# A diffusion step with product-key experts: three small groups of work change their place in a hand-written order

## The reference, cut to what matters

```python
def layer(x, cond, h0_f, h0_b, rows, p):
    ...
    y, h_f, h_b = token_mixer(h, h0_f, h0_b, rows, p)     # w_in, SSM | conv, rms norm per conv head, w_out
    x = x + g1 * y
    h = rmsnorm(x, p["norm2_g"]) * (1 + sc2) + sh2
    x = x + g2 * peer(h, p["w_query"], p["sub_keys"], p["expert_u"], p["expert_v"])

def block(xb):                                            # 128 tokens, 8 heads, 16 experts of each
    q = (xb @ w_query).astype(jnp.float32).reshape(TOKEN_BLOCK, PEER_HEADS, 2, PEER_DQ // 2)
    s = jnp.einsum("thse,sne->thsn", q, sk)
    ...                                                   # two top-16 of 128 keys, then top 16 of 256 sums
    hid = jnp.einsum("thkd,td->thk", expert_u[idx], xb).astype(jnp.float32)
    act = (jax.nn.gelu(hid) * gate).astype(xb.dtype)
    return jnp.einsum("thk,thkd->td", act, expert_v[idx])
```

## Time and profile before

| | |
|---|---|
| median of 3 runs | 1960.12 us |
| the three runs | 1955.56, 1960.12, 1962.29 us |
| span of the profiled execution, first to last instruction | 1954.5 us |
| own time of the profiled execution | not given apart from its span; the lowest run lies 1.1 us above the span, the median 5.6 us |
| busy: PE, DVE, ACT, POOL | 1197.1, 1423.2, 373.2, 717.9 us |
| moved by DMA | 745.91 MB, of them 671.13 MB by the gathers' queue |

### The profile page before, as it was taken

How to read it: one execution, slowest core, us unless ns; L and a number is a source line. 1 busy time by engine, 2 the same in 40 slices (tenths; PEclk the granted TensorE clock), 3 DMA queues, 4 the chain that set the end, 5 groups by cost and what they waited for, 6 DMA issues and landing times.

```text
span 1954.5 us, 22601 instructions
## 1 busy us (share of the span) xinstructions
PE 1197.1 (61%) x7716; PEld 476.1 (24%) x7716; DVE 1423.2 (73%) x3894; ACT 373.2 (19%) x845; POOL 717.9 (37%) x666
## 2 busy tenths in 40 slices
PE   6999888999767767774553434453444454444434
PEld 3569544444322322220110000111000011111001
DVE  8978557777766776667777777777777678877775
ACT  5242431221122111111211011121111111211010
POOL 0000233333333333334444444444444444344442
PEclk9999999999878777775755555565555565555555
DMA  8556799999999999999999999999999999999996
GB/s 347 179 196 220 275 358 401 373 396 415 401 368 374 404 414 401 397 401 393 421 421 422 419 410 416 412 412 412 416 413 415 417 412 415 415 410 419 412 409 254
DMA packets 126243, 745.91 MB, mean 382 GB/s; under 512 B 12128, under 2 KB 34912, under 8 KB 40624
## 3 DMA queue, kind: packets, MB, share of 16 engines
q0 software_dynamic: 92160, 671.13, 83.8%
q1 hardware_dynamic: 33968, 73.35, 10.5%
HBM read 741.78 MB, written 2.65 MB: 381 GB/s over the span
## 4 chain that ended last, share of the span: by engine, by line
DMA 33%; PE 30%; DVE 24%; issue 10%; ACT 1%; SPq 0%; DVEq 0%; POOL 0%; POOLq 0%; ACTq 0%
DMA r<-table,gidx 29%; DVE r L1707 8%; PE bank L846 7%; PE bank L814 6%; PE bank L951 3%; DMA r<-w_query 3%; PE bank L964 2%; PE bank L543 2%; DMA r<-w_u 2%; PE bank L781 1%; DVE wgt L1719 1%; DVE i L1649 1%; DVE r L1675 1%; DVE i L1655 1%; DVE r L1650 1%
## 5 line engine op out<-in xcount | busy, mean ns | idle before, releaser
L1890 POOL DMA_INDIRECT r<-table,gidx x640 | 709.7, 1109 | 1053.1 <-PE bank L846 891.0
L1707 DVE CUSTOM_DVE_ANT_0 r<-r 128x1024 f32<-128x1024 f32 x640 | 780.3, 1225 | 310.4 <-DMA r<-table,gidx 292.8
L846 PE MATMUL bank<-r,wgt 128*32 128x512 f32 x2560 | 532.2, 916 | 711.3 <-DVE wgt L1719 692.2
L846 PEld LDWEIGHTS bank<-r,wgt 128*32 128x32 f32 x2560 | 61.3, 130 | 1078.5 <-DVE wgt L1719 1011.3
L1258 ACT ACTIVATE r<-r 128x2 f32<-128x2 f32 x320 | 65.1, 204 | 1033.3 <-DVE r L1707 1016.4
L814 PE MATMUL bank<-hT_r,r 128*128 128x512 f32 x256 | 120.1, 624 | 0.9 <-ACT hT_r L1112 0.9
L1716 DVE TENSOR_TENSOR r<-r 128x2 f32<-128x2 f32 x320 | 50.1, 157 | 68.5 <-ACT r L1258 68.5
L1719 DVE TENSOR_TENSOR wgt<-fold,r 128x64 f32<-128x64 f32 x320 | 72.0, 225 | 11.1
L814 PEld LDWEIGHTS bank<-hT_r,r 128*128 128x128 f32 x256 | 50.0, 200 | 75.1 <-issue 75.1
L1258 ACT ACT_TABLE_LOAD x51 | 65.4, 1283 | 0.9
L964 PE MATMUL bank<-mix_r,r 128*128 128x512 f32 x128 | 61.0, 619 | 0.0
(11 more groups left out here) (356 smaller groups left out, 1438.5 us busy)
## 6 DMA issues: line engine op xcount, KB each, us to landing
r<-w_mod SPq DMA_DIRECT2D x24, 1024.0 KB, 8.2
r<-w_query SPq DMA_DIRECT2D x15, 1024.0 KB
r<-table,gidx POOLq DMA_INDIRECT x640, 11.7
r<-w_tiles SPq DMA_DIRECT2D x12, 512.0 KB, 8.2
x_r<-w_tiles SPq DMA_DIRECT2D x10, 512.0 KB, 5.9
hT_r<-xT SPq DMA_DIRECT2D x4, 640.0 KB, 5.9
r<-w_u SPq DMA_DIRECT2D x1, 2048.0 KB, 29.9
r<-w_o SPq DMA_DIRECT2D x1, 2048.0 KB, 10.9
```

The costliest lines, as they stand in the source:

```text
L846: last = mm(bank[ACC[b % 2][h]][to:to + TG, :], wgt[:, g % 2, e, :], rows[:, k % SLOTS, D + h * 512:D + (h + 1) * 512], start=(G % HEADS = ...
L1707: V.tensor_tensor_reduce(rows[:, s, 0:D], rows[:, s, 0:D], h2r[tg], 1.0, 0.0, ALU.mult, ALU.add, hid[:, par, k:k + 1]).then_inc(dot_done, 1)
L1890: G_.indirect_dma_start(rows[:, k % SLOTS, :], None, table, bass.IndirectOffsetOnAxis(gidx[:, e, k:k + 1], 0)).then_inc(row_in[k % SLOTS], 16)
```

## The change

There are three edits, all within the first block's heads.

1. On PE the conv heads' sums of squares (positions 12, 18, 24, 30) come ahead of the position's products of the projection instead of behind them.
2. On PE, for G of 1 to 5, the two halves of a query stand at g = 2 and 3 instead of 3 and 4, and the scores at g = 5 instead of 6. For G = 0 they stay.
3. On ACT the copy of the queries (g = 5) comes behind the position's gelu instead of ahead of it. The copy of the scores moves from ahead of the gelu of g = 6 to behind the gelu of g = 7.

```diff
@@ PE, latent_front(n)
+                if n in (12, 18, 24, 30):
+                    i = (n - 12) // 6
+                    pe.wait_ge(sql_ready, 5 + i)
+                    pe.wait_ge(mixl_ready, i + 1)
+                    for j in range(4):
+                        last = mm(bank[6][:, 2 * j:2 * j + 2], sql[i % 2][:, j * P:(j + 1) * P], headones[:, 0:P:64], start=True, stop=True)
+                    last.then_inc(sql_used, 1)
                 if n == 9:
                     spread_columns(0)
                 if n in (13, 19, 25, 31):
...
                     if half:
                         last.then_inc(zl_mm, 1)
-                if n in (12, 18, 24, 30):
-                    i = (n - 12) // 6
-                    pe.wait_ge(sql_ready, 5 + i)
-                    pe.wait_ge(mixl_ready, i + 1)
-                    for j in range(4):
-                        last = mm(bank[6][:, 2 * j:2 * j + 2], sql[i % 2][:, j * P:(j + 1) * P], headones[:, 0:P:64], start=True, stop=True)
-                    last.then_inc(sql_used, 1)
@@ PE, the loop over heads and positions
                     if u < HEADS:
-                        if g in (3, 4):
-                            query(u, (g - 3,))
-                        if g == 6:
+                        early = 1 if G else 0
+                        if g + early in (3, 4):
+                            query(u, (g + early - 3,))
+                        if g + early == 6:
                             scores(u)
@@ ACT, the loop over heads and positions
+                    gelu(G, e, g)
                     if u < HEADS:
                         if g == 5:
                             take_q(u)
-                        if g == 6:
+                        if g == 7:
                             take_scores(u)
-                    gelu(G, e, g)
```

## The result

The changed kernel takes 1970.81 us, the median of 9 runs (1962.04 to 1975.60). The kernel before takes 1959.51 us beside it, also 9 runs (1950.79 to 1962.44). The ratio is 1.0056, with a 95% interval of 1.0039 to 1.0072: 11 us slower, 7.6 to 14. The forecast of 1960 us was wrong, and 1970.8 lies above its range. It also lies above the 1967 us of the rival that ends slower.

A forecast was written before the change was run, and what follows sets the result against it. The gathers' DMA at 416 GB/s was taken as the bound, PE almost a second. Terms -3.5 - 1.0 + 4.7 + 0 = +0.2 us on a span of 1954.5 gave 1954.7; plus 5.6 to the median, about 1960 us, range 1952.5 to 1968.

The forecast's parts named there:

- Position 10: Query for G = 1: PE waits 3 to 5 us for its load, costing about 0, at worst 2 us.
- Position 26: Query for G = 3: PE waits 6.0 us for its load, then slow matmuls; net 4.7 us lost, bounds 0 and 8.
- position 3: Case in before's trace: PE waited 4.98 us for a query's load, matmuls took 3.78 us, DMA lost 6.6 us.
- Slow matmuls behind a wait: At position 26 the query's matmuls after the wait run on the slow clock, adding 1.8 us on PE.
- Edits 1 and 3: First block: waits for gelus and roots mostly go; DMA gains 4.5 us, at most 7.2, at least 0.
- the term of 3.5 us: DMA time gained by edits 1 and 3 from 320 to 380 us, taken between 2.4 and 6.0 us.
- Edit 2 in G = 2, 4 and 5: Moving these heads' queries up is neutral: same matmuls, and the load has already landed.
- Edit 3's late copy: Scores copied later on ACT may delay DVE in six heads; counted at nothing, 3.5 us if nothing hides it.
- The load was not in time: Rival: G = 3's load comes sooner, so edit 2 costs nothing; 1953 to 1955.6 us; chance 0.18 of faster by over 0.3%.
- The wait for the load is longer: Rival: at position 26 PE stands 8 to 9 us, other gains at their lower end; +6 to +8, 1967 us; chance 0.17.
- The edits move idle time only: Rival: idles change name, gain near 0, smaller loss at position 26; about +2, 1962 us; chance 0.65 together with middle case.

The follow-up runs named there:

- e9: The changed kernel with the queries early only in G = 1; 1960.77 us, ratio to before 1.0016.
- e7: The changed kernel with the queries early only in G = 2, 4 and 5; 1956.35 us, ratio to before 0.9990.
- e2: The kernel before with edit 2 alone (queries and scores one position up for G from 1 on); 1963.91 us, ratio to before 1.0042.
- e8: The changed kernel with the queries early only in G = 3; 1960.55 us, ratio to before 1.0012.
- e1: The changed kernel with edit 2 undone, edits 1 and 3 kept; 1955.32 us, ratio to before 0.9993.
- e3: The kernel before with edit 3 alone (ACT's copies behind the gelus); 1953.59 us, ratio to before 0.9986, without one run of 2622.91 us.
- e12: The changed kernel with edit 2 undone and the w_query loads for G = 1 and G = 3 issued earlier, a repeat run; 1950.57 us, ratio to before 0.9945.
- e13: The kernel of e6 run again, on the same chip as e12; 1955.11 us, ratio to before 0.9966.
- e6: The changed kernel with only the w_query loads for G = 1 and G = 3 issued earlier, queries still early; 1954.79 us, ratio to before 0.9990.

## Why the prediction was wrong, point by point

**Position 10, counted at nothing: this step failed.** The prediction said that the wait there "eats what edits 1 and 3 gained by then and costs about nothing: 0, at worst 2", because "DMA is full there (405 GB/s), with three positions of gathers in flight". The trace of before had DMA full because an add freed slots every 6 us. Adds 9 and 10 started 6 us apart (294.07 and 300.20); now they start at 288.16 and 302.22, 14.1 us apart. The wait of 2.94 us is the smaller part of the growth. The query itself moved in between the two adds (3.12 us), and the projection took 4.87 us instead of 3.60. POOL stood 12.30 us without a slot, which the gathers in flight did not cover: they lasted until about 300 us. Alone (e9 against e7) the place costs 5.1 us, or 4.6 by the means, give or take 3. It isn't the same in every execution: in e2's trace the wait was 0.89 us. I had reckoned the same shape of stall in full at position 26, from position 3, and dismissed it at position 10 by a window's mean that belonged to the order without it.

**Position 26: mechanism right, size about right.** Forecast were a wait of 6.0 us, matmuls of 3.78 us and slots free at 412.0. The trace has 6.64, 3.78 and 412.4. The forecast price was 4.7 us net; e8 against e7 measures 4.3, give or take 3. The gross loss of DMA around it was larger, 8.7 us where I had taken 6.6 from position 3. That isn't owed to arrears from position 10, for `e8_query_at_3`, which has none, loses nearly as much:

```profile
398.00:413.00 15.00, 10.15 (x43) 6.51 (x44) 6.47 (x16) 0.41 (x2) 1.87 (x2) 0.77 0.50 191
```

That is 15 x (1 - 191/416) = 8.1 us.

**Slow matmuls behind a wait.** They came at both places, 3.12 and 3.78 us instead of 1.95, with granted clocks of 0.67 and 0.50 in the 5 us behind the landings; 0.50 is the 1.2 GHz level. By the rule of the Trainium skill, "TensorE: Matmul & The Clock Gate", section "Why this matters for your kernels", that idle gaps between bursts are paid for with the slow clock, the trace agrees. I had put this on PE's sum at position 26 and left it out at position 10.

**Edits 1 and 3: the waits went as forecast, the gain in DMA time is not shown to be theirs.** ACT's idle of 5.83 us ahead of the scores went, the waits for gelus and roots fell from 33.7 to 6.4 us, and 320 to 380 us came to 392 GB/s. By bytes that is 60 x (392 - 368)/416 = 3.5 us, what the sum said, but the agreement is luck: e2, without edits 1 and 3, has 397 GB/s there. So the term of 3.5 us was read from a dip that edit 2 alone also removes, or that belongs to before's execution; which of the two is open. The whole gain forecast was 4.5 us, and e1 measures 1.4 (interval from 4.7 faster to 2.0 slower), e7 2.0. The forecast is inside e1's interval and the middle lies lower.

**Edit 2 in G = 2, 4 and 5, counted at nothing: right as far as measured.** e7 and e1 agree to 0.0003, on two chips, each with an interval of about 0.0015 either way. **Edit 3's late copy, counted at nothing with 3.5 us as the other end: right for the time.** DVE's waits for it came in all six heads, 8.0 us in sum, and e3, with 10.5 us of them, is no slower than before.

**The rivals.** The load was not in time: it took 28.51 and 30.17 us. The page "DMA: Bandwidth & Descriptors" of the Trainium skill, section "Queues, rings and completion order", has the engines take turns between queues, and I had worked out that the load would speed up once gathers run out. The windows show why this didn't help: DMA stands at 404 to 415 GB/s until the landing at 299.13 and falls to 160 behind it. The gathers ran out after the load, not ahead of it, so no run here shows whether it would speed up without them. "The wait for the load is longer" came nearest in time but not in cause. In the changed kernel the wait was 6.64 us and not 8 (7.75 in e2); the missing time was at the other load, which I had looked at and priced at nothing. "The edits move idle time only" fits edits 1 and 3 by time, since the 1.4 us of e1 are not clear of nothing; it leaves out position 10 as the sum did.

**The sum with measured terms**: -2.0 for edits 1 and 3 with the neutral heads, +4.3 at position 26 and +5.1 at position 10 make +7.4 us, against +0.2 forecast and +11.3 measured (7.6 to 14). The rest, some 4 us, is within the intervals of the four kernels and isn't assigned. Nor are the two places only waits: e12 and e13 put the cost of early queries without any late load at 4.7 us (2 to 7), part of which the sum had at nothing.

## What to carry to other kernels

When a matmul moves ahead of the instruction that frees buffers, count the whole time between two such releases (the moved work, its wait, the slow clock behind it), and set that against how long the transfers in flight last. A window that is full in the old order says nothing of how much delay it can bear. Look up which load the moved instruction needs and how late it lands at every place where it is moved, and move the load first; it shares a queue, so look at the next load behind it as well. Then ask whether the move gains anything with its load in time: here it didn't, and moving the loads alone was the better change.

## What the runs showed of the hardware

How long a load of 1 MB on SP's queue takes beside the gathers is no constant. Beside the two of 28.51 and 30.17 us, the changed kernel's loads of `w_query` issued at 226.56, 325.88, 417.98 and 470.63 us took (KB, then us to landing):

```profile
r<-w_query SPq DMA_DIRECT2D x1, 1024.0 KB, 15.3
...
r<-w_query SPq DMA_DIRECT2D x1, 1024.0 KB, 20.9
...
r<-w_query SPq DMA_DIRECT2D x1, 1024.0 KB, 14.2
...
r<-w_query SPq DMA_DIRECT2D x1, 1024.0 KB, 29.8
```

The chain that ended last shows only loads that something waited for, so it shows the long ones (25 to 30 us) and hides the others. The three loads of 28 us and more were issued right behind another load of SP's list, as was that of 20.9; those of 15.3 and 14.2 were not. Moved up in e6, the two late ones took 13.9 and 12.8 us. What sets the time was not taken apart.

Slow matmuls came behind short waits too: the query took 3.12 us instead of 1.95 behind a wait of 2.94. The clock had been low a little earlier as well, 0.69 from 290 to 295, where the projection took 4.87 us. Waits of 0.87 and 1.93 us in e1 left the query at 2.05.
